# A feed-forward fed with the un-normalised residual: weight gain in the split, 1/rms applied to the product

## The reference

```python
def rmsnorm(x, w):
    xf = x.astype(jnp.float32)
    y = xf * lax.rsqrt(jnp.mean(jnp.square(xf), axis=-1, keepdims=True) + EPS)
    return (y * w.astype(jnp.float32)).astype(x.dtype)

# hybrid_layer, from its mixer's outputs on
    h = h + jnp.concatenate([o_gla, o_swa], axis=-1) @ w_out
    f = rmsnorm(h, norm_ff_w)
    return h + jnp.square(jax.nn.relu(f @ w_ff1)) @ w_ff2     # 1024 -> 4096 -> 1024
```

## Time and profile before

| | |
|---|---|
| median of 3 runs | 2263.61 us (2255.86 to 2266.65) |
| profiled execution: span from first to last instruction | 2263.9 us |
| PE busy | 2108.8 us (93%) |
| DVE busy | 1163.3 us (51%) |
| ACT busy | 783.6 us (35%) |
| POOL busy | 405.1 us (18%) |
| mean granted clock of TensorE | 0.939 |

### The profile page before, as it was taken

The page is one execution under the profiler, slowest core; times in us unless marked ns, Lnnn a source line. Parts: engine busy times, 40 slices in busy tenths (PEclk is TensorE's granted clock), DMA queues, the critical chain, the costliest instruction groups (busy, mean ns, idle before and its releaser), DMA issues.

```text
span 2263.9 us, 25698 instructions
## 1 busy us (share of the span) xinstructions
PE 2108.8 (93%) x9635; PEld 1682.8 (74%) x9635; DVE 1163.3 (51%) x1714; ACT 783.6 (35%) x1343; POOL 405.1 (18%) x339
## 2 busy tenths in 40 slices
PE   6996699599999999999999999998899998999996
PEld 4985567388888878888887887776566776888885
DVE  6137523776766574544445425546533655444443
ACT  3132243232222342222224235555645633222222
POOL 2000003999996010000000000004100000000000
PEclk9887667799999989999999999999999999999998
DMA  4221003466664313333334443332312532333331
GB/s 126 63 75 43 1 0 109 143 206 193 213 204 148 102 47 93 93 93 101 101 94 108 121 121 112 109 101 72 110 56 75 186 112 66 93 93 99 101 96 46
DMA packets 274887, 233.60 MB, mean 103 GB/s; under 512 B 16423, under 2 KB 248226, under 8 KB 274264
## 3 DMA queue, kind: packets, MB, share of 16 engines
q1 hardware_dynamic: 254960, 164.19, 25.0%
q0 software_dynamic: 18224, 62.91, 8.9%
q10 hardware_dynamic: 1624, 5.45, 1.1%
HBM read 215.41 MB, written 12.58 MB: 101 GB/s over the span
## 4 chain that ended last, share of the span: by engine, by line
PE 81%; DVE 11%; ACT 4%; issue 2%; DMA 0%; ACTq 0%; POOL 0%; SPq 0%; DVEq 0%
PE bank L965 24%; PE bank L967 23%; PE bank L966 23%; PE bank L1145 1%; PE bank L1327 1%; DVE wlo L1478 1%; DVE arena L1635 1%; ACT whi L479 1%; PE bank L1395 1%; DVE arena L1518 1%; PE bank L1237 1%; PE bank L1181 1%; DVE xlo L1484 1%; PE bank L1413 1%; DVE arena L1503 1%
## 5 line engine op out<-in xcount | busy, mean ns | idle before, releaser
L965 PE MATMUL bank<-xhi,whi 128*128 128x512 f32 x1768 | 708.6, 401 | 50.3 <-DVE xlo L1484 38.7
L966 PE MATMUL bank<-xlo,whi 128*128 128x512 f32 x1768 | 699.3, 396 | 0.0
L967 PE MATMUL bank<-xhi,wlo 128*128 128x512 f32 x1768 | 698.7, 395 | 0.0
L1478 DVE TENSOR_TENSOR wlo<-stage,whi 128x1024 fp32r<-128x1024 f32 x309 | 393.5, 1285 | 288.4 <-ACT whi L479 288.0
L479 ACT ACTIVATE whi<-stage 128x1024 fp32r<-128x1024 f32 x309 | 321.2, 1050 | 442.3 <-PE bank L967 415.7
L965 PEld LDWEIGHTS bank<-xhi,whi 128*128 128x128 f32 x1768 | 338.6, 192 | 138.3 <-issue 36.9
L967 PEld LDWEIGHTS bank<-xhi,wlo 128*128 128x128 f32 x1768 | 338.6, 192 | 72.3
L966 PEld LDWEIGHTS bank<-xlo,whi 128*128 128x128 f32 x1768 | 339.4, 192 | 67.9
L1747 DVE SCALAR_TENSOR_TENSOR H<-bank,sc,H 128x512 f32<-128x512 f32 x304 | 220.3, 749 | 86.1 <-PE bank L967 86.0
L965 PE MATMUL bank<-hidhi,whi 128*128 128x512 f32 x608 | 239.7, 394 | 2.7 <-DVE hidlo L1772 2.7
L967 PE MATMUL bank<-hidhi,wlo 128*128 128x512 f32 x608 | 236.8, 389 | 0.0
(11 more groups left out here) (388 smaller groups left out, 2165.8 us busy)
## 6 DMA issues: line engine op xcount, KB each, us to landing
arena<-in_w_ada POOLq DMA_DIRECT2D x72, 512.0 KB, 4.0
stage<-in_w_in SPq DMA_DIRECT2D x71, 512.0 KB, 3.8
stage<-in_w_ff SPq DMA_DIRECT2D x64, 512.0 KB, 4.6
stage<-in_w_gate SPq DMA_DIRECT2D x44, 512.0 KB, 4.5
stage<-in_w_up SPq DMA_DIRECT2D x44, 512.0 KB, 3.8
stage<-in_w_down SPq DMA_DIRECT2D x44, 512.0 KB, 3.8
stage<-in_w_out SPq DMA_DIRECT2D x16, 512.0 KB, 4.0
arena<-arena ACTq DMA_DIRECT2D x16, 256.0 KB, 5.6
```

What stands on the lines that cost most here:

```text
L965: mm(out, sh, mh, start=start, stop=False, **kw)
L966: mm(out, sh, ml, start=False, stop=False, **kw)
L967: return mm(out, sl, mh, start=False, stop=stop, **kw)
L1478: V.tensor_tensor(wlo[:, static % SPLITS, :], stage[:, static % STAGES, :], whi[:, static % SPLITS, :].bitcast(F32), ALU.subtract).then_in ...
```

## The change

Relu and a positive factor can be exchanged: relu((H x weight x rstd) @ w) = relu((H x weight) @ w) x rstd. The change splits H x weight without rstd and applies rstd to the product.

- ACT rounds H x weight straight from H (the weight as the instruction's scale), DVE forms the remainder from H, weight and `xhi` in one instruction; `u0` is not used here. The split has nothing to do with the variance and stands ahead of it in both queues. ACT's square of tile 7 stands after the rounding of tile 1.
- TensorE's variance matmuls stand behind chunk 0 (`after_first`) and no longer ahead of it. Root and reciprocal follow, and DVE's reciprocal stands ahead of the first weight remainder of group 0.
- ACT's relu goes in all 16 groups. DVE forms max(bank, 0) x rstd into `act_t`, and then `act_t` x `act_t` into `hid_t`: one DVE instruction more per hidden tile. ACT squares `act_t` as before, and waits for DVE's first instruction.
- POOL starts its modulation sums when `x_ready` is 24, which is when the new split is done.

```diff
--- before.py
+++ after.py
@@ -482,12 +482,12 @@
             for c in range(AHEAD):
                 hi(c)
 
-            def split_hi(n, kt, src, shift=0.0):
+            def split_hi(n, kt, src, shift=0.0, gain=1.0):
 
                 if n > 0 and kt == 0:
                     act.wait_ge(chunk_done, split_last[n - 1] + 1)
                 if isinstance(shift, float):
-                    ins = A_(xhi[:, kt, :], src, ACT.Copy)
+                    ins = A_(xhi[:, kt, :], src, ACT.Copy, scale=gain)
                 else:
                     ins = A_(xhi[:, kt, :], src, ACT.Identity, bias=shift)
                 ins.then_inc(s("x_rounded"), 1)
@@ -542,7 +542,7 @@
                     act.wait_ge(s("um_ready"), 1)
                     A_(mhi[:, :, :], um[:, :, :], ACT.Copy).then_inc(s("um_rounded"), 1)
 
-            split_seq = {k: n for n, k in enumerate([0, 1, 3, 4, 5])}
+            split_seq = {k: n for n, k in enumerate([0, 3, 4, 5])}
 
             norm(0)
 
@@ -693,8 +693,6 @@
 
                 hi(*chunk(0))
                 for j in range(2):
-                    act.wait_ge(chunk_done, 4 * g + (C_FF1 + j + 1))
-                    A_(act_t[j], bank[j][:, :], ACT.Relu).then_inc(act_fn, 1)
                     act.wait_ge(act_fn, 2 * g + (j + 1))
                     A_(hidhi[:, j, :], act_t[j], ACT.Square).then_inc(hid_rounded, 1)
                     hi(*chunk(1 + j))
@@ -715,7 +713,15 @@
                 if not last:
                     hi(*chunk(5))
 
-            norm(1, KT - 2)
+            square(1, KT - 2)
+            for kt in range(KT):
+                act.wait_ge(H_added, norm_H[1] + kt + 1)
+                split_hi(split_no[1], kt, H[:, kt, :], gain=pc("norm_ff_w", kt))
+                if kt == 1:
+                    square(1, KT - 1)
+            A_(small[:, 255:256], eps[:, 0:1], ACT.Sqrt)
+            act.wait_ge(s("sq_used"), sq_used_end[1])
+            A_(std, bank[7][:, :], ACT.Sqrt, scale=1.0 / D, bias=eps[:, 0:1]).then_inc(s("std_ready"), 1)
             ffn1_group(0, lambda j: (C_FF1 + j + AHEAD,))
             with act.Fori(0, (G_FF1 - 1) // 3 - 1) as i:
                 for m in range(3):
@@ -1189,7 +1195,7 @@
                     pe.wait_ge(H_added, n - 3)
                 project(c, bank[n % 4][:, :], filling=1 if n == 0 else None).then_inc(chunk_done, 1)
 
-            def ffn_group(g, base, per, hb, hid0, first, filling=None, static=None, before_down=None):
+            def ffn_group(g, base, per, hb, hid0, first, filling=None, static=None, before_down=None, after_first=None):
 
 
                 n1 = per - 2
@@ -1199,6 +1205,8 @@
                         pe.wait_ge(H_added, g * 8 + (hb - 8 + 4 + j + 1))
                     project(c0 + j, bank[j][:, :], static=st + j, filling=filling if j == 0 else None)\
                         .then_inc(chunk_done, 1)
+                    if j == 0 and after_first is not None:
+                        after_first()
 
                 def down(j, x):
 
@@ -1223,8 +1231,7 @@
 
             HID0 = {"FF1": 0, "FFA": 2 * G_FF1, "FFB": 2 * G_FF1 + 2 * G_FF2}
 
-            norm(1, [(s("sw_mix"), NB)])
-            ffn_group(0, C_FF1, 4, H_base["FF1"], 0, True, 2, C_FF1)
+            ffn_group(0, C_FF1, 4, H_base["FF1"], 0, True, 2, C_FF1, after_first=lambda: norm(1, [(s("sw_mix"), NB)]))
             with pe.Fori(0, (G_FF1 - 1) // 3) as i:
                 for m in range(3):
                     ffn_group(i * 3 + (1 + m), C_FF1, 4, H_base["FF1"], 0, False, None, C_FF1 + 4 + 4 * m)
@@ -1478,9 +1485,12 @@
                 V.tensor_tensor(wlo[:, static % SPLITS, :], stage[:, static % STAGES, :],
                                 whi[:, static % SPLITS, :].bitcast(F32), ALU.subtract).then_inc(chunk_lo, 1)
 
-            def split_lo(n, kt, src, shift=None):
+            def split_lo(n, kt, src, shift=None, gain=None):
                 dve.wait_ge(s("x_rounded"), 8 * n + kt + 1)
-                if shift is None:
+                if gain is not None:
+                    ins = V.scalar_tensor_tensor(out=xlo[:, kt, :], in0=src, scalar=gain, in1=xhi[:, kt, :].bitcast(F32),
+                                                 op0=ALU.mult, op1=ALU.subtract)
+                elif shift is None:
                     ins = V.tensor_tensor(xlo[:, kt, :], src, xhi[:, kt, :].bitcast(F32), ALU.subtract)
                 else:
                     ins = V.scalar_tensor_tensor(out=xlo[:, kt, :], in0=src, scalar=shift, in1=xhi[:, kt, :].bitcast(F32),
@@ -1509,7 +1519,7 @@
                     before_use()
                 gain = {3: lambda kt: gain23[:, kt:kt + 1], 4: lambda kt: gscale[:, 8 + kt:9 + kt],
                         5: lambda kt: gscale[:, 16 + kt:17 + kt]}.get(k) or (lambda kt: pc(norm_g[k], kt))
-                seq = {0: 0, 1: 1, 3: 2, 4: 3, 5: 4}[k]
+                seq = {0: 0, 3: 1, 4: 2, 5: 3}[k]
                 m = {3: 0, 4: 3, 5: 6}.get(k)
                 for kt in range(KT + 1):
                     if kt < KT:
@@ -1757,11 +1767,14 @@
                 lo(*chunk(0))
                 for j in range(2):
 
-                    dve.wait_ge(act_fn, g * 2 + (hid0 + j + 1))
                     if per == 4:
-                        V.scalar_tensor_tensor(out=hid_t[j], in0=bank[j][:, :], scalar=0.0, in1=act_t[j],
-                                               op0=ALU.max, op1=ALU.mult).then_inc(hid_f32, 1)
+                        dve.wait_ge(chunk_done, g * per + (base + j + 1))
+                        V.scalar_tensor_tensor(out=act_t[j], in0=bank[j][:, :], scalar=0.0, in1=rstd,
+                                               op0=ALU.max, op1=ALU.mult).then_inc(act_fn, 1)
+                        dve.wait_ge(act_fn, g * 2 + (hid0 + j + 1))
+                        V.tensor_tensor(hid_t[j], act_t[j], act_t[j], ALU.mult).then_inc(hid_f32, 1)
                     else:
+                        dve.wait_ge(act_fn, g * 2 + (hid0 + j + 1))
                         dve.wait_ge(chunk_done, g * per + (base + 2 * j + 2))
                         V.tensor_tensor(hid_t[j], bank[2 * j + 1][:, :], act_t[j], ALU.mult).then_inc(hid_f32, 1)
                     if per == 4:
@@ -1778,7 +1791,9 @@
 
             unit = lambda x: one_col
             ffn_chunk = lambda c: (c,)
-            norm(1)
+            for kt in range(KT):
+                split_lo(split_no[1], kt, H[:, kt, :], gain=pc("norm_ff_w", kt))
+            rstd_of(1)
             ffn_group(0, C_FF1, 4, unit, lambda j: (C_FF1 + j + AHEAD,))
             with dve.Fori(0, (G_FF1 - 1) // 3 - 1) as i:
                 for m in range(3):
@@ -2072,7 +2087,7 @@
             for j, name in enumerate(("lambda_q1_2", "lambda_k1_2", "lambda_q2_2", "lambda_k2_2")):
                 pool.dma_start(tl(25)[:, 64 * j:64 * j + 64], t[name].to_broadcast([P, 64])).then_inc(s("const_loaded"), 16)
             pool.wait_ge(s("silu_c"), 1)
-            pool.wait_ge(x_ready, 16)
+            pool.wait_ge(x_ready, 24)
             ring = [s(f"ada_in{i}") for i in range(3)]
             total = 9 * KT
```

## The result

The change made the kernel slower: 2299.45 us in the median of 4 runs (2294.01 to 2308.01), beside 2265.13 us (2255.86 to 2266.91). The ratio is 1.0154, with a 95% interval of 1.0124 to 1.0184. The forecast was 2244 us.

What follows compares the result with a forecast made beforehand. TensorE was taken to bound most of the span, standing idle in the seam. The terms -24.7 + 4 + 1 = -19.7 took the span from 2263.9 to 2244.2 us, predicted as 2244, range 2233 to 2257.

Steps and rivals of the forecast that it cites:

- The seam: Between output projection and first feed-forward, through group 0: idle TensorE time shrinks, a gain of 24.7 us.
- bad end: Seam's low case: POOL adds catch both DVE chains of group 0 and the clock falls, gain 22.5 us.
- rival 3: Seam shortens less: both chains caught, clock down in both gaps, 9.5 us lost in groups; 2252 us, chance 0.06.
- The groups: Remaining 15 groups of the first feed-forward: POOL adds stretch DVE's chain, +4 us, between -2.3 and 9.5.
- my own sign of being wrong: In the 15 groups: the prediction is wrong if TensorE waits over 12 us.
- Rival 2: DVE's feed-forward queue gives the gain back: 1.9 us per group (28.5 us) or 4.3 (64 us, 2304); chance 0.04.
- The spare: In each group, hidden tile 1's DVE chain was said to have 0.5 us spare before TensorE waits.
- POOL late: POOL's later modulation sums end at 775 and meet the next norm's squares, +1 us (0 to 14).
- The 7 us: In the feed-forward groups, DVE's new squares hold POOL's sums up by 7 us, at most 22.
- +4 against +1: Groups' cost with the new square reading two SBUF inputs, +4 us, against about +1 with one from PSUM.

Runs made afterwards that it cites:

- e3: The kernel before with one line of the change, POOL starting at x_ready 24 behind the seam's split: 2253 us, ratio 0.9932.
- POOL short: POOL's scales and adds cut to 8 of 1024 columns: 2234 us in the changed kernel, 2243 us in the kernel before.
- e4: The kernel before plus one idle DVE product per hidden tile, both inputs in SBUF, result unread: 2282 us, ratio 1.0077.
- e5: The kernel before plus one idle DVE product per hidden tile, one input from PSUM, result unread: 2289 us, ratio 1.0097.
- e10: As e3, but the f32 hidden tile is written to a free PSUM bank, where the remainder reads it: 2240 us, ratio 0.9885.
- e1: The changed kernel with DVE's new square taking one input from PSUM (one factor 1/rms left out): 2246 us, ratio 0.9902.
- e11: As e4, but the remainder waits for the idle product's end by a semaphore: 2316 us, ratio 1.0222.

## Why the prediction was wrong

- **The seam.** Forecast 24.7 gained, measured 21.7, just under the bad end (22.5). As in that end, tile 0's chain was caught, and TensorE stood 4.94 us behind chunk 1. The clock fell after the first gap already (0.66 from 419 to 424), which of the forecast's cases only rival 3 had: chunk 0 took 7.2 us instead of 5.4. The pace of the remainders (0.66 to 0.68) was as stated. What I had credited to the new order belongs to POOL's start: e3 has the same seam without it, and with POOL short the order is worth 4 us.
- **The groups: the step that failed.** Above, "an add of 2.4 is met with 0.5 spare in a third of 15 groups" gave at most 9.5, and I took +4. Measured +52.3, with 38.1 us of TensorE's waiting where 12 was my own sign of being wrong. Rival 2, which had 0.04, has the mechanism that came, at 3.5 us per group, between its two prices. I had treated the meeting with an add as a matter of chance, once in three groups. It is none: DVE and POOL alternate, and each wait of DVE puts its next instruction close to POOL's next. In the twelve groups beside POOL, 22 of 24 squares, 23 of 24 remainders and 22 of 47 weight remainders were held up, by 81 us in sum; before, in eleven groups, 10 of 22 remainders and 18 of 45 weight remainders, by 26. The weight remainder that stands between the two tiles' chains carries the waits of tile 0 into tile 1. I had written that down, and then counted the 3 waits of TensorE in 11 groups as evidence against it, where the rows of DVE had 10 remainders held up already.
- **The spare.** 0.5 us was too much. In e4 and e5, groups without POOL take 22.15 us instead of 21.76: an instruction that lengthens the chain by 0.6 costs 0.4, so 0.2 was to be had.
- **POOL late.** Forecast +1, its sums ending between 768 and 790. They ended at 761.3, 70 us early. The 7 us by which the squares were to hold POOL up did not come: its scales and adds took 261 us in sum, before 271. The sentence that a square waits for the add "and then mostly fills the pause that POOL makes for its next DMA" was right: the square of 459.43 ends at 460.23, between the add's end at 459.68 and the scale of 460.61. But the remainder behind it, for which no pause is left, then waits for that scale. In e3 and e10, where POOL starts 8 us later, its sums do meet the next norm.
- **The rule on two inputs.** What the Trainium skill says in SBUF — State Buffer, "Who interferes with whom", of DVE instructions with two SBUF inputs and with one held in every trace: between 370 and 800 us of all fourteen, DVE's 128x512 instructions with an input from PSUM took 0.68 to 0.75 us, with POOL or without. I had put 3 us on the square's second SBUF operand (+4 against +1); e1 makes it 54.

## What to carry to other kernels

Where POOL and DVE work side by side, count the contending instructions (both inputs in SBUF) of each DVE chain, and see at what point of POOL's cycle each one arrives once the first has waited: the phase is not random. One wait can cost up to a whole POOL instruction, and what stands behind in the queue inherits it. Give such an instruction an input from PSUM, by writing the intermediate tile to a free bank, before taking instructions away. Try the one-line parts of a change alone: here one line had the gain of the seam, and another the loss of the groups.

## What the runs showed of the hardware that I had not expected

- 0.1 us decides whether a DVE instruction with two SBUF inputs waits for POOL. With POOL's next scale 0.93 us off, 42 of 42 that started 0.37 to 0.48 us after the end of POOL's add passed; of 22 that started 0.58 to 0.78 us after it, 20 waited, mostly 1.3 us. Between e4 and e11 a semaphore wait between two instructions makes this difference (1.57 and 0.68 us without it, 2.13 and 2.02 with it).
- The same program can spread: e4 gave 2269 to 2289 us in six executions, while e10, where of these forms only the weight remainders still contend, stayed within 2237 to 2242. That the phase against POOL is what differed is argued, since only one execution of e4 was traced.
- DVE instructions that read from and write to PSUM cost the same 0.69 to 0.70 us as from SBUF at 128x512.
